# A one-core encoder block on Trainium2: x in columns from the host, the output product by halves with an early gather, and the first attention's scores in row halves

## The reference, cut to what matters

```python
h = rmsnorm(x, norm1_g)
z = h @ w_in                     # q, k, v of mixer A; c_q, c_kv, k_rope of mixer B; two gates
o_a = dilated_mixture(qa, ka, va)            # 8 heads of 64
o_b = mla(c_q, c_kv, k_rope, ...)            # 8 heads of 64 + 32
merged = sigmoid(gate_a) * (o_a @ w_a_out) + sigmoid(gate_b) * (o_b @ w_b_out)
x = x + merged @ w_o                         # the output product and the residual
h2 = rmsnorm(x, norm2_g)
logits = h2 @ w_router + b_router            # 32 experts, the best 4 of each token, softmax over them
x = x + sum over the chosen experts of gate * expert(h2)
out = rmsnorm(x, final_g)
```

## Time and profile before

| | |
|---|---|
| median of three runs | 1134.14 us |
| the profiled execution's own time | 1134.09 us |
| its span, first to last instruction | 1132.3 us |
| around the span | 1.79 us |
| PE busy | 1091.9 us, 96% |
| DVE, ACT, POOL busy | 223.8, 125.4, 30.3 us |
| DMA moved | 434.61 MB, mean 384 GB/s |
| chain that ended last | PE 65%, DMA 32% |

### The profile page before, as it was taken

The page is one execution under the profiler, slowest core; times in us unless marked ns, Lnnn a source line. Parts: engine busy times, 40 slices in busy tenths (PEclk is TensorE's granted clock), DMA queues, the critical chain, the costliest instruction groups (busy, mean ns, idle before and its releaser), DMA issues.

```text
span 1132.3 us, 12526 instructions
## 1 busy us (share of the span) xinstructions
PE 1091.9 (96%) x5278; PEld 482.5 (43%) x5279; DVE 223.8 (20%) x549; ACT 125.4 (11%) x271; POOL 30.3 (3%) x43
## 2 busy tenths in 40 slices
PE   7999999999999999999999999999999999999996
PEld 5858887443333333333333333333333333333332
DVE  1264213331111111111111121111111111111112
ACT  1053111210000000000000010000000000000001
POOL 1250000000000000000000000000000000000000
PEclk9999999999999999999999999999999999999999
DMA  9934366399999999999999999999999999999995
GB/s 362 411 144 168 130 222 233 144 396 421 432 432 432 429 431 433 431 432 433 432 431 431 435 428 429 439 428 429 438 428 431 435 429 431 434 429 431 417 421 232
DMA packets 31484, 434.61 MB, mean 384 GB/s; under 512 B 6944, under 2 KB 7200, under 8 KB 9440
## 3 DMA queue, kind: packets, MB, share of 16 engines
q1 hardware_dynamic: 26960, 430.33, 90.1%
q10 hardware_dynamic: 4496, 3.87, 1.1%
HBM read 433.14 MB, written 1.05 MB: 383 GB/s over the span
## 4 chain that ended last, share of the span: by engine, by line
PE 65%; DMA 32%; DVE 1%; ACT 1%; issue 0%; POOL 0%; DVEq 0%; SPq 0%; POOLq 0%
DMA ring<-in_up 32%; PE ps L1352 26%; PE ps L1366 11%; PE ps L1172 5%; PE ps L1300 3%; PE ps L1374 3%; PE ps L1186 2%; PE ps L1249 2%; PE ps L1061 2%; PE ps L1361 2%; PE ps L1116 1%; PE ps L1080 1%; PE ps L1051 1%; PE ps L1336 1%; PE ps L1330 1%; PE ps L1089 1%
## 5 line engine op out<-in xcount | busy, mean ns | idle before, releaser
L1352 PE MATMUL ps<-ring,work 128*64 128x512 f32 x2048 | 470.7, 605 | 20.2 <-DMA ring<-in_up 20.2
L1352 PEld LDWEIGHTS ps<-ring,work 128*64 128x64 f32 x2048 | 141.8, 138 | 317.8 <-issue 283.8
L1366 PE MATMUL ps<-ring,work 128*64 128x512 f32 x1024 | 226.8, 595 | 1.6 <-DVE work L977 1.6
L918 DVE TENSOR_SCALAR work<-ps 128x512 f32<-128x512 f32 x32 | 22.1, 691 | 698.1 <-PE ps L1352 698.1
L1366 PEld LDWEIGHTS ps<-ring,work 128*64 128x64 f32 x1024 | 70.6, 137 | 133.7 <-issue 128.0
L1300 PEld LDWEIGHTS ps<-work 128*128 128x128 f32 x512 | 61.8, 191 | 24.0 <-issue 22.7
L1300 PE MATMUL ps<-work 128*128 128x128 f32 x512 | 70.3, 281 | 0.5 <-DVE work L904 0.5
L1374 PE MATMUL ps<-work 64*128 64x512 f32 x264 | 65.6, 615 | 0.7 <-ACT work L658 0.7
L1172 PE MATMUL ps<-work,ring 128*128 128x256 f32 x256 | 56.6, 379 | 0.0
L631 ACT ACTIVATE work<-ps 128x256 f32<-128x256 f32 x33 | 12.7, 383 | 355.5 <-PE ps L1336 355.5
L1172 PEld LDWEIGHTS ps<-work,ring 128*128 128x128 f32 x256 | 48.5, 190 | 6.6
(11 more groups left out here) (157 smaller groups left out, 520.9 us busy)
## 6 DMA issues: line engine op xcount, KB each, us to landing
ring<-in_up SPq DMA_DIRECT2D x52, 4096.0 KB, 45.2
ring<-in_down SPq DMA_DIRECT2D x26, 4096.0 KB, 44.1
ring<-in_up SPq DMA_DIRECT2D x48, 1024.0 KB, 10.8
ring<-in_down SPq DMA_DIRECT2D x24, 1024.0 KB, 10.6
ring<-in_front SPq DMA_DIRECT2D x22, 1024.0 KB, 17.2
ring<-in_front SPq DMA_DIRECT2D x2, 832.0 KB, 7.5
ring<-in_x SPq DMA_DIRECT2D x2, 512.0 KB, 4.2
ring<-in_x ACTq DMA_DIRECT2D x1, 1024.0 KB, 4.8
```

The source lines that it names most:

```text
L918: return dve.tensor_scalar(up_c, ps[:, UP, :], LIMIT, -LIMIT, ALU.min, ALU.max)
L1352: last = pe.matmul(ps[n * CAP:(n + 1) * CAP, bank, :], x, w[bank - GATE][:, n * BANK:(n + 1) * BANK], start=k == 0, stop=k == KT - 1, skip ...
L1366: last = pe.matmul(ps[n * CAP:(n + 1) * CAP, Y, :], lhs(actT, k), w[:, n * BANK:(n + 1) * BANK], start=k == 0, stop=k == KT - 1, skip_grou ...
```

## The change: what it does

**Start.** The host also gives x transposed (`x_cols`) and g as columns (`g1_cols`). `x_cols` is loaded straight to `hT` in two halves, around the first latent slot, which is loaded in two pieces. DVE and ACT multiply by g in place, and PE starts the latent products on columns that are not yet divided by the root mean square. The rows of x are still loaded, behind these; their squares give the factor per token. The factor is applied afterwards: to the latent results in DVE's small operations, and to `hT`, before q and k, as a row that PE spreads over the partitions with two products (ones times a diagonal matrix) ahead of the last latent block; DVE multiplies `hT` by it in four operations of 128x512. The 16 transposes go.

**Mixer A's scores.** q is stored without zeros (`qT`; two DVE operations of 128x512 instead of four of 64x512, and no clearing by POOL). `scores_a(p)` makes both heads of a pair: four products of 256 columns, each over 64 rows, alternately rows 0 to 63 and 64 to 127, into two PSUM banks. It stands once for each pair, behind the turning of the even head. DVE's maximum of head k now waits for the turning of head k-2.

**The output product.** A slot of `wo` holds four row blocks of one column half. The order of the products is tile 0 left, tile 1 left, tile 0 right, tile 1 right. The routing's steps are placed anew between them. Counts, places and picks are made for each token tile by itself (`first_picks`), and tile 0's gather stands before tile 1's choice. Three of the four `open_sums` move into the first expert. SP issues the first four loads of turn 1 ahead of its wait for `opened` and slot 23.

```diff
-    slots += list(rows_of(w_o, 2))
+    for half in range(2):
+        slots += list(rows_of(w_o[:, half * BANK:(half + 1) * BANK], 4))
...
+            sp.dma_start(hT[:, 0:4, :], x_cols[:, 0:4, :]).then_inc(s_xT[0], 16)
+            dst, src = front[0]
+            sp.dma_start(dst[:, 0:2 * LATENT], src[:, 0:2 * LATENT]).then_inc(s_half, 16)
+            sp.dma_start(dst[:, 2 * LATENT:], src[:, 2 * LATENT:]).then_inc(loaded[0], 16)
+            sp.dma_start(hT[:, 4:8, :], x_cols[:, 4:8, :]).then_inc(s_xT[1], 16)
...
+            for at in range(4):
+                fine_load(1, at)
             sp.wait_ge(opened, 1)
             expert_load(0, 23)
...
-            for at in range(RING):
+            for at in range(4, RING):
                 fine_load(1, at)
...
-            pool.wait_ge(hT_ps, 4)
-            pool.memset(qmT, 0.0).then_inc(cleared, 1)
...
+            dve.wait_ge(s_g1, 16)
+            for j in range(2):
+                dve.wait_ge(s_xT[j], 16)
+                for k in (4 * j, 4 * j + 1):
+                    dve.tensor_scalar(hT[:, k, :], hT[:, k, :], g1[:, k:k + 1], None, ALU.mult).then_inc(hT_v, 1)
...
+            for t in range(TT):
                 dve.wait_ge(power, t + 1)
-                dve.tensor_scalar(xs[:, t, :], xrow[:, t, :], sums[:, 2 + t:3 + t], None, ALU.mult).then_inc(xs_ready, 1)
+                dve.tensor_scalar(diag[:, t, :], ident, sums[:, 2 + t:3 + t], None, ALU.mult).then_inc(diag_ready, 1)
+
+            dve.wait_ge(row_ready, 1)
+            for j in range(4):
+                dve.wait_ge(*((hT_read, 1), (freed, 1), (hT_read, 2), (freed, 2))[j])
+                dve.tensor_tensor(hT[:, 2 * j:2 * j + 2, :], hT[:, 2 * j:2 * j + 2, :], ps[:, 6, 0:SEQ].unsqueeze(1).to_broadcast([P, 2, SEQ]),
+                                  ALU.mult).then_inc(hT_normed, 1)
...
+            def first_picks(t):
+
+                dve.wait_ge(chosen_ready, t + 1)
+                dve.wait_ge(count_done, t + 1)
+                stepped(dve.scalar_tensor_tensor(out=struck[:, t, 0:E], in0=counts[:, t * E:(t + 1) * E], scalar=1.0, in1=chosen[:, t, :],
+                                                 op0=ALU.add, op1=ALU.mult))
...
             choose(0)
-            residual(1, 0)
...
             residual(1, 1)
+            first_picks(0)
             dve.wait_ge(x2_sq, 4)
             mean_square(1).then_inc(ms, 1)
             choose(1)
             normed(1, 0)
...
+            first_picks(1)
+            normed(1, 1)
...
+            def scores_a(p):
+
+                for t in range(TT):
+                    for o in range(2):
+                        rows = slice(o * HD, (o + 1) * HD)
+                        last = pe.matmul(ps[:, o, t * SEQ:(t + 1) * SEQ], qT[rows, p, t * P:(t + 1) * P], kT[rows, p, :], start=True, stop=True)
...
             pe.wait_ge(pick_ready, 1)
-            gather_first()
-            open_sums(1, 1).then_inc(opened, 1)
+            gather_first(0, range(0, 2))
+            add_parts(1)
+            gather_first(0, range(2, 8))
+            pe.wait_ge(chosen_ready, 2)
...
+            open_sums(0, 0)
+            pe.wait_ge(pick_ready, 2)
+            gather_first(1, range(0, 4)).then_inc(gathered_low, 1)
+            gather_first(1, range(4, 8)).then_inc(gathered, 1)
```

More of the change, by code:

```diff
@@ L737, in _ @@
+            step_wait()
             for t in range(TT):
@@ L874, in normed, with build_places @@
                                          op0=ALU.mult, op1=ALU.mult).then_inc(h2_ready, 1)
+            def build_places(r):
+                return dve.tensor_scalar(places[:, :, r * E:(r + 1) * E], struck[:, :, 0:E], -float(1 + CAP * r), None, ALU.add)
+            def first_picks(t):
[3 more added lines that the diff above has]
+                                                 op0=ALU.add, op1=ALU.mult))
+                step_wait()
+                stepped(dve.tensor_scalar(places[:, t, 0:E], struck[:, t, 0:E], -1.0, None, ALU.add))
+                step_wait()
+                for b in range(PAIR):
+                    last = dve.tensor_scalar(pick[:, t, b * CAP:(b + 1) * CAP], slots, places[:, t, b:b + 1], None, ALU.is_equal)
+                last.then_inc(pick_ready, 1)
             residual(0, 0)
+            take_x2T(0)
+            residual(1, 0)
+            take_x2T(1)
             residual(0, 1)
-            take_x2T(0)
-            dve.wait_ge(x2_sq, 2)
+            dve.wait_ge(x2_sq, 3)
             mean_square(0).then_inc(ms, 1)
+            dve.wait_ge(power, 4)
+            normed(0, 0)
+            normed(0, 1)
             choose(0)
-            residual(1, 0)
-            normed(0, 0)
-            take_x2T(1)
-            normed(0, 1)
             residual(1, 1)
+            first_picks(0)
             dve.wait_ge(x2_sq, 4)
@@ L1139, in _ @@
                     turn_probs(k)
-                    if k + 2 < HEADS:
-                        scores(k + 2)
+                    if k % 2 == 0 and k + 2 < HEADS:
+                        scores_a(p + 1)
                 if p == 0:
@@ L1247, in project @@
             def project(t, k, n):
-                w = slot(FIRST["wo"] + k // 2, 2, D)
-                return pe.matmul(ps[:, 4 + 2 * t + n, :], gateT[:, k, t * P:(t + 1) * P], w[:, k % 2, n * BANK:(n + 1) * BANK],
+                w = slot(FIRST["wo"] + 2 * n + k // 4, 4, BANK)
+                return pe.matmul(ps[:, 4 + 2 * t + n, :], gateT[:, k, t * P:(t + 1) * P], w[:, k % 4, :],
                                  start=k == 0, stop=k == KT - 1)
+            counts = ps[:, GATE, P:P + (TT + 1) * E]
             for k in range(KT):
-                if k % 2 == 0:
-                    arrived(FIRST["wo"] + k // 2)
+                if k % 4 == 0:
+                    arrived(FIRST["wo"] + k // 4)
                 pe.wait_ge(merged, k + 1)
-                for n in range(2):
-                    last = project(0, k, n)
+                last = project(0, k, 0)
                 if k == 0:
@@ L1261, in _ @@
             last.then_inc(wo_done, 1)
+            for k in range(KT):
+                last = project(1, k, 0)
+                if k % 4 == 3:
+                    last.then_inc(freed, 1)
+                if k == 3:
+                    turn_rows(0, 0)
             pe.wait_ge(router_ready, 1)
@@ L1406, in experts @@
                         up_tile(homes(pair, k // 4)[:, b, k % 4, :], k, use(k), up_done).then_inc(freed, 1)
-                        if static and e == 0 and k == 1:
+                        if static and e == 0 and k in (0, 1, 2):
+                            last = open_sums(*((0, 1), (1, 0), (1, 1))[k])
+                            if k == 2:
+                                last.then_inc(opened, 1)
+                        if static and e == 0 and k == 3:
                             pe.wait_ge(first_gates, 1)
-                            turn_gated(1).then_inc(first_ps, 1)
+                            turn_gated(1, Y).then_inc(first_ps, 1)
                         if k == 5:
@@ L1496 @@
     nc = bacc.Bacc("TRN2", target_bir_lowering=False, num_devices=1, dynamic_dma_scratch_size=1024)
-    given = {name: np.ascontiguousarray(inputs[name]) for name in INPUTS}
+    given = {"x": np.ascontiguousarray(inputs["x"])}
+    given["x_cols"] = np.ascontiguousarray(np.asarray(inputs["x"])[0].T.reshape(KT, P, SEQ).transpose(1, 0, 2))
+    given["g1_cols"] = np.ascontiguousarray(np.asarray(inputs["norm1_g"])[0].reshape(KT, P).T)
+    given.update({name: np.ascontiguousarray(inputs[name]) for name in INPUTS[1:]})
     given["front"] = pack_front(*(np.asarray(inputs[name])[0] for name in FRONT_WEIGHTS))
```

206 lines of the change are left out of this document (100 added, 106 removed).

## The result

| | before | after |
|---|---|---|
| median, us (20 runs each, same chip) | 1134.12 | 1136.23 |
| ratio, 95% interval | | 1.0019 [1.0012, 1.0025] |
| first latent product / q and k begin | 11.02 / 23.49 | 7.16 / 20.50 |
| first scores | 55.21 | 56.18 |
| first expert (T) / its down part | 232.79 / 253.22 | 232.12 / 256.17 |

The change made the kernel 2.1 us slower; I had said 7.1 faster. The profiled execution of the changed kernel took 1140.98 (span 1139.1), 4.8 above its median, so it is read for places, and sizes come from the timed runs. T fell by 0.7 us where 8.7 were forecast. Of its 20 timed runs the nine up to 1136.05 have a mean granted clock of 0.989 to 0.991 (median 1134.70) and the eleven from 1136.08 up 0.984 to 0.988 (median 1137.31), so part of the 2.1 us goes with the clock.

A forecast was written before the change was run, and what follows sets the result against it. The stream of expert weights, started by slots PE frees, was taken to set the end. Start -3.8, scores -2.4, output product to first expert -2.5 and stream +1.6 gave -7.1: 1127.0 us from 1134.09, range 1123.0 to 1131.5.

The forecast's parts named there:

- What bounds the kernel: Whole kernel: the stream of expert weights sets the end, started by slots PE frees; PE waited 20.2 us for `in_up`.
- The start: Up to q and k: first latent product at 5.8, q and k at 19.7 instead of 23.5; gain 3.8 us.
- the price of the first four frees: First expert: frees 1.83+1.0 us apart, an `open_sums` between; five loads landed by T+17.4 instead of T+15.8.
- The stream's term: Weight loads behind T: the stream is 1.6 us late relative to T, bounds 0.8 and 5.3.
- Output product to first expert: From the last output product to the first expert: 9.1 us instead of 11.6, gain 2.5, bounds 1.0 and 3.5.
- my second rival: Start: pace doubles 2.6 us after the first latent product, gain 4.8 instead of 3.8, time 1126.0; chance 0.20.
- The scores: Mixer A: a pair's scores take 0.97 to 1.07 us instead of 1.73; gain over four pairs taken as 2.4.
- The third: Before T: PE waits for bias tables and latent weights landing at DMA's time; -1 left, 1133; chance 0.07.
- The fourth: First expert: slot 23 and first frees meet a dry queue, stream loses 5.3, T moves 2.4; 1137.0; chance 0.04.

The follow-up runs named there:

- the output product alone: Kernel before with only the output product by halves, the early gather and the new place of sums and loads; 1137.42 us, ratio 1.0017.
- the openings ahead of the gather again: Changed kernel with three openings of the sums ahead of the wait for tile 1's places, the fourth behind the gather, load order kept; 1136.37 us, ratio 1.0020.
- the router loads late: Changed kernel with ScalarE's loads of the router's weights and bias issued behind the squares of the latents instead of ahead; 1133.46 us, ratio 0.9988.
- the part alone: Kernel before with only the new start (x in columns, latents first, factor as a row); 1134.97 us, ratio 1.0006.
- the bias-first run: Changed kernel with ScalarE loading the router's bias before the router's weights, both ahead of the latent squares; 1136.16 us (one run).
- g1_cols on SP: Changed kernel with the load of g1_cols issued by SP, behind the first half of x_cols, instead of by ScalarE; 1132.71 us, ratio 0.9990.

## Why the prediction was wrong

**What bounds the kernel** was right: PE's waits for `in_up` stay near where they were, as the page's row has it,

```profile
L1401 PE MATMUL ps<-ring,work 128*64 128x512 f32 x2048 | 474.3, 608 | 21.2 <-DMA ring<-in_up 21.2
```

for 20.2; the end follows the stream, and the stream follows the front.

**Two steps failed.** Of the 9.2 us between forecast and result, the start holds 4.4: its sum put ScalarE's loads ahead of the squares at nothing, without a row (below, "The start"). The output product and the stream hold 3.9, and this second step is the sentence that PE work added behind T costs nothing while PE has 20 us of waits to spare, with T as the time by which the stream goes. The waits are real, but they lie behind 651 us, and up to 300 the stream lives on the slots that PE frees. What stood behind T delayed these: the down part starts 2.95 later than in the kernel before and its first load is issued at 258.14 for 255.19. I had the price of the first four frees (five loads by T+17.4; the trace has 243.24+6.8 = 250.0 = T+17.9), but not the second hole. The stream's term was 1.6; in the output product alone it is 3.0 + 0.6 = 3.6 us (2.5 by the ratio), T having fallen from 232.79 to 232.16. How much of it belongs to the openings and how much to the place of slot 23 is not shown: with the openings ahead of the gather again 2.5 us of loss are left. My second miss in the same place: two of the openings stood where PE would else wait for DVE, and were free there. Moving them uncovered waits of PE; in the run that moved three of them (1139.61) T came later.

**Output product to first expert**, -2.5 said. T - start of the product is 41.00 (232.12-191.12) for 41.39 (232.79-191.40): 0.4. Of the missing 2.1 the gather at the granted clock of 0.50 explains 1.3 (2.91-1.58): with the router loads late it runs at full pace and the same stretch is 39.57 (227.91-188.34), a gain of 1.8, within my bounds of 1.0 to 3.5.

**The start**, -3.8 said, bounds -6.1 to -2.2. The trace shows 3.0 up to q and k: the first product waits for `in_front` to 7.16, not 5.8, and the latents take 13.34 us for my 13.9. In the seven other executions with this start the first product comes at 6.58 to 7.26 and the latents take 13.5 to 14.6, so the gain is 1.8 to 3.4. The mechanism was right and the size 0.4 to 2.0 too large; the 12.9 us of my second rival are reached in none. I counted DVE's and POOL's work beside q and k but went through no row of ScalarE's loads, though the kernel before has one of 3.69 us right ahead of the squares. It cost 1.99 of waiting and 1.7 at a lower pace (5.30-3.60), 3.7 in all, which turns the 3.0 gained into the 1.0 lost at the first scores but for 0.3, and the part alone is +0.6. The lower pace is not in every run: with the openings ahead the wait is 1.37 and v runs at full pace. In the kernel with all three parts it costs 2.8 to 3.0 at the end (1136.23-1133.46, or +2.1 for -0.9).

**The scores**, -2.4 said, -1.5 measured. The pair takes 1.07, as worked out. But a round (69.84 to 76.19 before, 69.74 to 75.70 after) gains 0.39, not 0.66: from start to start the turning ahead of the row halves takes 0.59 for 0.49 before, the row halves up to the next turning 1.17 for 1.07, and the turning behind them 0.49 for 0.44. In the last round PE waits 0.66 for DVE, for 0.20 before. From the first scores to mixer B's it is 36.92 for 38.17, a gain of 1.25. The change of tiling was priced inside the eight instructions, and part of it falls on their neighbours. In the Trainium skill "TensorEngine Tiling (Array Packing)", Key Properties, says that a change of tiling mode drains TensorE. The 0.10 in the row ahead of the change agrees with it; no run shows that this is its cause.

**The rivals.** The third, early time given back before T, came nearest in the start, by another cause than the tables. The fourth had the right sign and mechanism (slot 23 and the first frees in a dry queue); I gave it 0.04 because it needed three terms at their ends, while two larger things stood in none of my cases. That its 1137.0 lies near the measured 1136.2 is luck: it has T 2.4 sooner and the stream 5.3 later, and the result is 0.7 and 2.8. By terms of the forecast: start 4.4 off, scores 0.9, product and stream together (-0.9 for +3.0) 3.9, sum 9.2.

## What to carry over

Where a stream of loads sets the end, count megabytes moved up to a fixed time beside the time of the first consumer, and look for holes at every gap in which PE frees no slot, the second one too. An instruction that fills a wait is free only where it stands; price what its place uncovers as well as what it adds elsewhere. A change of what is loaded at the start asks for every issue on every queue that compute shares, since an engine that issues a load can be held by it.

## What was not expected of the hardware

- One 16 KB load on ScalarE's queue held the engine for 19.35 to 20.35 us in six kernels, where the kernel before shows 3.69, and 0.46 when issued one place earlier.
- After short waits of PE its granted clock fell to 0.50 (1.2 for 2.4 GHz): behind the wait of 1.99 at 50 us, and in the gather, behind waits of 0.41 and 0.69 among small products. The windows of the changed kernel (the third number from the right is the clock):

```profile
52.00:54.00 2.00, 2.00 (x3) 0.67 (x2) 0.31 (x1) 0.00 (x0) 1.92 (x3) 0.50 1.03 417
...
226.00:228.00 2.00, 2.00 (x11) 2.00 (x11) 1.68 (x8) 1.32 (x3) 0.00 (x0) 0.50 1.01 426
```

  It doesn't always fall: in the changed kernel with its router loads late the same twelve instructions run at full pace (1.58), behind the same waits of 0.41 and 0.69. And the kernel before has eight waits of 2.1 to 2.2 us for `in_up` between 698 and 1049: behind five of them sixteen instructions take 5.35 us, behind three 3.65. What decides was not tried.
- The profiled execution of the changed kernel has one such stretch late, at a wait for `in_up`:

```profile
1052.41 6.48 PE L1401 MATMUL ps<-ring,work 128*64 128x512 f32 x16 [3.33 <-DMA ring<-in_up]
```

  Sixteen instructions take 6.48 us for 3.65 elsewhere, 2.8 lost. The execution of the bias-first run has the same stretch (6.37 us behind a wait of 3.58, at 1048.03), the one with g1_cols on SP has a wait as long (3.65) and full pace behind it (3.65 us). With the stretch taken off, the first two executions come to what their streams ask for (4.1 for 4.2, and -0.6 for -0.7), so it is taken as a part of the 4.8 by which this execution lay above the median; no run shows that directly.
